# A three-block transformer forward pass: the last unit of expert weights in sixteen transfers of 15 to 1 and 8 rows

## What is computed

```
def expert_choice_ffn(h, router, w_gate, w_up, w_down):
    B, S, D = h.shape
    cap = CAPACITY_FACTOR * S // N_EXPERTS            # 2 * 256 // 16 = 32
    aff = jax.nn.softmax(jnp.einsum('bsd,de->bse', h, router).astype(jnp.float32), axis=-1)
    vals, idx = lax.top_k(aff.transpose(0, 2, 1), cap)
    xg = jax.vmap(lambda hb, ib: hb[ib])(h, idx)
    hid = jax.nn.silu(jnp.einsum('becd,edf->becf', xg, w_gate)) * jnp.einsum('becd,edf->becf', xg, w_up)
    y = jnp.einsum('becf,efd->becd', hid, w_down) * vals[..., None].astype(h.dtype)
    return jax.vmap(lambda ib, yb: jnp.zeros((S, D), yb.dtype).at[ib.reshape(-1)].add(yb.reshape(-1, D)))(idx, y)

...
        x = x + expert_choice_ffn(rms_norm(x, norm_ffn[l]), router[l], exp_gate[l], exp_up[l], exp_down[l])
    return rms_norm(x, norm_final)
```

## Time and profile before

| | |
|---|---|
| median of 3 runs | 1742.86 us (1737.71 to 1745.14) |
| the profiled execution | 1742.7 us, span 1740.9 us |
| mean granted TensorE clock | 0.951 of full speed |
| PE busy | 1560.2 us, 90% of the span |
| VectorE / ScalarE busy | 815.8 us (47%) / 378.3 us (22%) |
| moved by DMA | 386.37 MB, 222 GB/s over the span |

### The profile page before, as it was taken

The page is one execution under the profiler, slowest core; times in us unless marked ns, Lnnn a source line. Parts: engine busy times, 40 slices in busy tenths (PEclk is TensorE's granted clock), DMA queues, the critical chain, the costliest instruction groups (busy, mean ns, idle before and its releaser), DMA issues.

```text
span 1740.9 us, 26417 instructions
## 1 busy us (share of the span) xinstructions
PE 1560.2 (90%) x10938; PEld 1088.5 (63%) x10938; DVE 815.8 (47%) x1685; ACT 378.3 (22%) x952; POOL 2.1 (0%) x6
## 2 busy tenths in 40 slices
PE   9999999999999999999999999999999757656655
PEld 6877888884488787888648778999853212112111
DVE  6676467665576765766646467564521000000001
ACT  4362131110325422311002561111211000000001
POOL 0000000000000000000000000000000000000000
PEclk9999999999999999999999999999999888688787
DMA  9324335444542242544444322121898999999998
GB/s 394 131 74 162 129 125 207 161 177 171 204 170 98 92 175 73 201 178 154 185 175 147 119 97 81 69 76 52 341 386 351 427 425 423 425 424 425 424 421 329
DMA packets 50050, 386.37 MB, mean 222 GB/s; under 512 B 5648, under 2 KB 6160, under 8 KB 10384
## 3 DMA queue, kind: packets, MB, share of 16 engines
q1 hardware_dynamic: 47952, 375.16, 54.2%
q10 hardware_dynamic: 1984, 9.57, 1.4%
HBM read 383.65 MB, written 1.05 MB: 221 GB/s over the span
## 4 chain that ended last, share of the span: by engine, by line
PE 74%; DMA 19%; ACT 2%; DVE 2%; SPq 2%; issue 1%; DVEq 0%; ACTq 0%
PE ps L239 53%; DMA arena<-in_stream 7%; DMA par<-in_stream 7%; DMA ring<-in_stream 4%; PE ps L2390 3%; PE ps L1128 2%; PE ps L1615 2%; DMA const<-in_stream 1%; PE ps L243 1%; PE ps L1216 1%; SPq L3824 1%; PE ps L776 1%; PE ps L1276 1%; PE ps L1249 1%; SPq L3792 1%
## 5 line engine op out<-in xcount | busy, mean ns | idle before, releaser
L239 PE MATMUL ps<-arena 128*128 128x256 f32 (+4 forms) x2364 | 525.5, 480 | 84.1 <-DMA arena<-in_stream 73.3
L239 PEld LDWEIGHTS ps<-arena 128*128 128x128 f32 (+1 forms) x2364 | 307.6, 171 | 259.3 <-issue 114.4
L239 PE MATMUL ps<-ring,arena 128*128 128x256 f32 (+5 forms) x1172 | 323.0, 508 | 40.8 <-DMA ring<-in_stream 36.3
L239 PEld LDWEIGHTS ps<-ring,arena 128*128 128x128 f32 (+1 forms) x1172 | 178.8, 176 | 160.4 <-issue 78.3
L239 PE MATMUL ps<-arena,ring 128*128 128x256 f32 (+1 forms) x1140 | 236.1, 355 | 0.0
L239 PEld LDWEIGHTS ps<-arena,ring 128*128 128x128 f32 x1140 | 191.6, 192 | 29.5 <-issue 9.9
L3071 DVE TENSOR_TENSOR arena<-arena,ps 128x512 f32<-128x512 f32 x8 | 5.5, 687 | 298.9 <-PE ps L2849 298.9
L2849 PE MATMUL ps<-arena 128*32 128x512 f32 x218 | 134.2, 743 | 0.0
L1163 ACT ACTIVATE arena<-arena,small 128x256 f32<-128x256 f32 x112 | 55.7, 498 | 45.5 <-DVE small L1145 45.1
L239 PE MATMUL ps<-arena,spare 128*128 128x128 f32 x510 | 65.5, 278 | 0.0
L239 PEld LDWEIGHTS ps<-arena,spare 128*128 128x128 f32 x510 | 60.4, 192 | 0.7
(11 more groups left out here) (474 smaller groups left out, 2007.7 us busy)
## 6 DMA issues: line engine op xcount, KB each, us to landing
ring<-in_stream SPq DMA_DIRECT2D x131, 1024.0 KB, 4.9
arena<-in_stream SPq DMA_DIRECT2D x111, 1024.0 KB, 15.7
arena<-in_stream SPq DMA_DIRECT2D x24, 2048.0 KB, 36.4
ring<-in_stream SPq DMA_DIRECT2D x12, 2048.0 KB, 31.7
spare<-in_stream SPq DMA_DIRECT2D x5, 2048.0 KB, 39.0
par<-in_stream SPq DMA_DIRECT2D x8, 1024.0 KB, 38.2
const<-in_stream SPq DMA_DIRECT2D x8, 1024.0 KB, 38.5
spare<-in_stream SPq DMA_DIRECT2D x6, 1024.0 KB, 8.0
```

The lines of the kernel that those rows point to most:

```text
L239: ins = self.pe.e.matmul(out, lhsT, rhs, start=start, stop=stop)
```

## The change

The last unit is no longer issued by `expert_unit`. After the same wait, SP issues sixteen transfers into the same slot, one behind the other, of 15, 14, 13 and so on down to 1 row and then of 8 rows, 128 in all. Each adds 16 to the slot's semaphore, and PE's wait for this unit asks for 15 times 16 more.

```
+LAST_ROWS = [*range(15, 0, -1), 8]
+assert sum(LAST_ROWS) == P
...
-        self.pe.e.wait_ge(self.loaded[first], self.bases[first] + 16 * len(slot_parts(self.slots[first])) * loads)
+        parts = len(LAST_ROWS) - 1 if s == EXPERT_UNITS - 1 else 0
+        self.pe.e.wait_ge(self.loaded[first], self.bases[first] + 16 * (len(slot_parts(self.slots[first])) * loads + parts))
...
-            for s in range(EXPERT_SLOTS + 1, EXPERT_UNITS):
+            for s in range(EXPERT_SLOTS + 1, EXPERT_UNITS - 1):
...
+            s = EXPERT_UNITS - 1
+            e.wait_ge(p.expert_slots_used, unit_ahead(s) + 1)
+            at, u = 0, DENSE_UNITS + s
+            for rows in LAST_ROWS:
+                e.dma_start(p.expert_slots[slot_of(s)][at:at + rows, :], stream[u * P + at:u * P + at + rows, :]).then_inc(
+                    p.expert_slot_loaded[slot_of(s)], 16)
+                at += rows
```

## The result

Over 20 runs each the changed kernel took 1746.09 us (1743.03 to 1749.97) and the kernel before 1742.04 us (1737.71 to 1745.81). The ratio is 1.0025, with a 95% interval of 1.0017 to 1.0033: **4.4 us slower, 3.0 to 5.7**. The profiled execution is one of the quick ones of its kernel, 1743.3 us with a span of 1741.5, so what follows compares intervals within it and not its span.

A forecast was written before the change was run, and what follows sets the result against it. The weight stream bounds the last fifth, and the last unit's landing sets the end. Issues 0, wait 0, rows and completions -0.8 made 1741.9 from the profiled 1742.7, or 1742.0 us in terms of the median; range 1738.5 to 1749.0.

The forecast's parts named there:

- What bounds the end: End of the run: weight stream bounds it; from the last unit's landing at 1731.55 everything follows, 9.3 us to the end.
- the cap by the unit before the last: PE's wait for the last unit: an earlier landing gains at most 1.4 us, then the last unit but one decides.
- Issues and PE's wait at nothing: SP's sixteen issues, 5.3 to 6.9 us, done by 1710.3, covered by 14.6 us; PE still waits once: both cost nothing.
- Completions at 0.1 us: DMA engines: up to fifteen more completions each, taken as 0.1 us in all, with an upper bound of 7.5 us.
- Which engine moves what: Last unit's rows: n-row parts use the same first n engines, giving 16 rows down to none instead of 8; +2.5 to -2.5 us.
- rows and completions -0.8: Last unit on the DMA engines: 0.9 us gained by redistributing rows, less 0.1 for completions.
- If the seven early engines are the first ones: DMA tail: engines done at about 1727.4 take the extra rows, ending by 1729.9; the late six lose rows, gain 1.1 us.
- rival A: DMA tail: late engines are the first ones or lie mixed and get more rows; +2.5 us, 1745.4; chance 0.2.
- Rival B: SBUF writes: engines writing neighbouring partitions share a way, a row takes 0.62 us; +3.8 us, 1746.6, up to 1750.2; chance 0.35.
- The likeliest case: Whole kernel: the forecast of 1742.0 us, chance 0.35, equal to the chance of Rival B, yet kept.
- B needs a limit that no row shows: Reason given for keeping the forecast over Rival B at equal chance 0.35: no profile row shows sharing at the destination.
- The range: Whole kernel's time: 1738.5 to 1749.0 us, leaving out Rival B's upper end; within 0.5% of before at chance 0.91.

## Why the prediction was wrong, step by step

- **What bounds the end**: right. Landing of the last units, then a chain of fixed length; the cap by the unit before the last was named, for a gain. That this unit could itself come late was not; "if the landing of the units before the last moves too" stands in the text as what would make me wrong, and it is what happened.
- **Issues and PE's wait at nothing**: right that they cost nothing, since the queue was far ahead. The size was wrong: sixteen issues took 9.45 us and not 5.3 to 6.9, one of them 4.08 us. That they were done at 1710.46, against 1710.3 forecast, is luck: SP began 2.4 us earlier in this execution.
- **Completions at 0.1 us**: in keeping with the runs. Eight per engine cost nothing (0.9993), and the upper bound of 7.5 us was too wide.
- **Which engine moves what**: the count was right. Parts of 8 rows ran on eight engines, at a DMA share of 0.51. By the rule that I cited from the Trainium skill, DMA: Bandwidth & Descriptors, "Why a DMA increments its semaphore by 16 and not by 1", this is what follows, and the trace agrees.
- **The failed step** is the term "rows and completions -0.8", and it failed in both of its premises. The one that decided the changed kernel's time is that a row goes on taking 0.31 us, at all engines and with the unit in front untouched. A row took 0.50 us at the median and up to 1.04, and the unit before the last, on which the chain now ends, came 3.7 us late. Uneven rows without neighbours left that unit on time (7.43 us after the mark, against 7.45). The other premise is "If the seven early engines are the first ones". No row had said so. With 16 rows each for the first eight, the last two landings lay 4.94 us apart, the time of 16 rows: a late engine was among the first eight. That alone is +2.5 us, rival A, where I gave 0.2.
- **Rival B** gave 1746.6; 1746.09 was measured. Its mechanism, engines that hold each other up at the destination, is shown by 12 to 15 GB/s per busy engine in the changed kernel, by 15 and 16 GB/s against 26 for parts that are near or far in SBUF (wherever they lie in device memory), and by 221 against 418 GB/s for neighbouring against every second partition. The closeness of the number is luck, since the price was worked out for the wrong unit: I let sixteen rows take 0.62 us each on one engine. In fact the loss begins when the early engines come to their neighbouring rows, while the late ones are still writing the unit before. "A row takes twice as long" was a fair guess: with parts of 16 rows the steady rates were 216 to 269 GB/s of 423, 1.6 to 2.0 times.
- The Trainium skill, SBUF — State Buffer, "Door 1: The DMA port swizzle", says that partitions 0 to 63 reach eight of sixteen ports and 0 to 127 all. The runs agree: 221 GB/s and 418. By its table 16 neighbours from partition 0 reach four ports, a quarter; an estimate from that and our 423 GB/s is 106 GB/s. The runs show 216 to 251 for such parts in a queue, and eight neighbours at the full rate of eight engines. So the page's figure for one part by itself is not the rate of many parts in a row.
- **The likeliest case**: the argument "B needs a limit that no row shows" was weighed the wrong way. No row showed the forecast's order of engines either. Where two unseen conditions stand against each other, the one with a stated mechanism deserved more than an equal chance. And a gain was capped at 1.4 us while a loss was not, so even equal chances spoke against the change.
- **The range** held the time, and within 0.5% was right.

## What to carry to other kernels

Read the quotient of rate and DMA share, not either alone: it tells engines that have nothing to do from engines that hold each other up. Of the ways to cut a transfer, two cost nothing here: by columns, and into even and odd partitions, the latter even for six units. Two halves of 64 neighbouring partitions made a 1742 us kernel 5.9 us slower. To spread a part over all of SBUF is not enough: parts of 16 rows, eight partitions apart, lost 13.1 us over six units. Engines that end at different times are no invitation to give them different loads, unless their numbers are known: here what a perfect division could win was 1.4 us, as far as PE could use it, and the uneven divisions that were tried cost 2.8 to 5.4 us.

## What the hardware showed that was not expected

- A transfer can slow the one in front of it. The unit before the last, whole and untouched, landed 3.7 us late with the changed one behind it, and the one in front of it was late as well: PE waited 2.63 us for it, where it had not waited before.
- With eight rows in each part, neighbouring partitions ran at 210 GB/s for eight engines, without loss in the steady state, while with sixteen rows the rate stayed at 216 to 251 GB/s for sixteen engines. At the start of the stretch the parts of eight do lose (188 GB/s at a share of 0.80, and the run with one unit). Why the loss passes in one case and not in the other is open.
- An issue on SP whose partitions are four apart took 0.66 us, and 0.34 us with neighbours, in the runs with six units. For parts of 64 KB with such steps that is the bound. In the one-unit run with 16 parts of 8 neighbours most issues took 0.57 us all the same, and in every one-unit run one issue took 3.2 to 6.3 us; neither is explained.
- PE was granted half its clock (0.50) for its last products in all runs with one unit where it had waited 2.97 us or more for the unit before the last or for the last, with 1.50 us for a group that took 0.85. The way from the last landing to the end was up to 1.4 us longer in these runs. It is not shown that the wait alone does it: with even and odd partitions the clock was half as well, after a wait of 1.39 us.
- Why engines that have had equal loads end 3.7 us apart was not tried.
